# Two networks in one kernel: the sequence and the context taken apart at both borders of the second network's first feed-forward

## The reference

```python
def reference(...):                    # cut
    x = first_block(x, mem, ...)       # retention + differential attention, cross attention, SwiGLU
    return second_block(x, ctx, ...)   # below

def _modnorm(x, g_pre, shift, scale):
    return _rmsnorm(x, g_pre) * (1 + scale) + shift
def _residual(x, y, g_post, gate, weight):
    return x + weight * gate * _rmsnorm(y, g_post)
def _swiglu(h, w1, w3, w2):            # 1024 -> 2816 -> 1024
    return (silu(h @ w1) * (h @ w3)) @ w2

# second_block: m, mc are nine vectors each, silu(c) @ w_ada + b_ada and silu(c_ctx) @ w_ada + b_ada
x     = _residual(x, _swiglu(_modnorm(x, g[0], m[0], m[1]), ffn1...), g[1], m[2], 0.5)
h_ctx = _residual(h_ctx, _swiglu(_modnorm(h_ctx, g[0], mc[0], mc[1]), ffn1...), g[1], mc[2], 0.5)
qa, ka, va, qn, qr, kn, kr, vb, ga, gb = _project(_modnorm(x, g[2], m[3], m[4]), ...)
_, cqa, cka, cva, ...                  = _project(_modnorm(h_ctx, g[2], mc[3], mc[4]), ...)
o_na  = _neighbourhood_attention(qa, ka, va, cka, cva, rpb, n_rows)   # window keys plus all context keys
...                                    # latent attention, gates, output projection
x     = _residual(x, y, g[3], m[5], 1.0)
x     = _residual(x, _swiglu(_modnorm(x, g[4], m[6], m[7]), ffn2...), g[5], m[8], 0.5)
```

## Time and profile before

| | us |
|---|---|
| median of 3 runs | 2569.59 |
| the three runs | 2557.73, 2569.59, 2571.56 |
| the profiled execution | 2560.82 |
| its span, first to last instruction | 2559.0 |
| busy: PE / DVE / ACT / POOL | 2372.7 / 891.6 / 862.8 / 1117.8 |
| mean granted TensorE clock, as a share of full speed | 0.973 |

### The profile page before, as it was taken

How to read it: one execution, slowest core, us unless ns; L and a number is a source line. 1 busy time by engine, 2 the same in 40 slices (tenths; PEclk the granted TensorE clock), 3 DMA queues, 4 the chain that set the end, 5 groups by cost and what they waited for, 6 DMA issues and landing times.

```text
span 2559.0 us, 33468 instructions
## 1 busy us (share of the span) xinstructions
PE 2372.7 (93%) x12008; PEld 1920.3 (75%) x12008; DVE 891.6 (35%) x1492; ACT 862.8 (34%) x1221; POOL 1117.8 (44%) x1352
## 2 busy tenths in 40 slices
PE   5998999878999979999999987999989998999997
PEld 4777677557888868888888866877856875788885
DVE  3332623376667572111110143234124444211113
ACT  3343534333222243311211233155434533422222
POOL 3433355067879763333333342333322033455543
PEclk8999999989999999999999999999999998999998
DMA  3221132234555531121111111122221011222222
GB/s 136 89 74 67 66 103 87 81 138 176 187 184 196 181 116 59 57 75 58 66 58 66 66 58 64 59 87 78 78 70 41 1 66 66 82 99 98 92 98 90
DMA packets 66604, 231.35 MB, mean 90 GB/s; under 512 B 7217, under 2 KB 9521, under 8 KB 66353
## 3 DMA queue, kind: packets, MB, share of 16 engines
q1 hardware_dynamic: 50224, 179.36, 20.1%
q10 hardware_dynamic: 16256, 50.21, 5.7%
HBM read 226.66 MB, written 2.10 MB: 89 GB/s over the span
## 4 chain that ended last, share of the span: by engine, by line
issue 38%; PE 33%; POOL 27%; DVE 1%; POOLq 0%; ACT 0%; DMA 0%; DVEq 0%; ACTq 0%; SPq 0%
PE ps L1405 27%; POOL WLO L293 27%; PE ps L1423 6%; DVE TN L1209 1%; POOLq L246 0%; DVE X L1213 0%; POOLq L291 0%; DVE Y L1235 0%; DMA RAW<-in_stream_dram 0%; PE ps L1474 0%; POOL X L305 0%; DVE TN L896 0%; DVE Y L1233 0%; ACT RS L692 0%; ACT RS L695 0%
## 5 line engine op out<-in xcount | busy, mean ns | idle before, releaser
L293 POOL TENSOR_TENSOR WLO<-RAW,WHI 128x256 fp32r<-128x256 f32 x1340 | 1105.6, 857 | 1399.3 <-ACT WHI L321 1398.5
L321 ACT ACTIVATE WHI<-RAW 128x1024 fp32r<-128x1024 f32 x335 | 354.6, 1059 | 763.1 <-DMA RAW<-in_stream_dram 727.3
L1405 PE MATMUL ps<-HLO,WHI 128*128 128x512 f32 (+2 forms) x1360 | 455.7, 368 | 11.3 <-DVE XK L1068 2.4
L1405 PE MATMUL ps<-HHI,WLO 128*128 128x512 f32 (+2 forms) x1360 | 449.8, 364 | 0.0
L1405 PE MATMUL ps<-HHI,WHI 128*128 128x512 f32 (+2 forms) x1360 | 447.9, 363 | 0.0
L1405 PEld LDWEIGHTS ps<-HLO,WHI 128*128 128x128 f32 (+1 forms) x1360 | 236.3, 188 | 61.2 <-issue 4.9
L1405 PEld LDWEIGHTS ps<-HHI,WHI 128*128 128x128 f32 (+1 forms) x1360 | 235.1, 188 | 44.4 <-issue 3.3
L1405 PEld LDWEIGHTS ps<-HHI,WLO 128*128 128x128 f32 (+1 forms) x1360 | 235.7, 188 | 41.0
L1423 PE MATMUL ps<-HHI,WHI 128*128 128x512 f32 x592 | 204.9, 381 | 52.9 <-POOL WLO L293 30.6
L1131 DVE TENSOR_TENSOR SF<-SF,ps 128x512 f32<-128x512 f32 (+1 forms) x66 | 51.3, 777 | 551.5 <-PE ps L1405 381.9
L1405 PE MATMUL ps<-GLO,WHI 128*128 128x512 f32 x704 | 227.7, 364 | 6.7 <-POOL WLO L293 3.7
(11 more groups left out here) (313 smaller groups left out, 3092.8 us busy)
## 6 DMA issues: line engine op xcount, KB each, us to landing
RAW<-in_stream_dram SPq DMA_DIRECT2D x335, 512.0 KB, 3.3
ADA<-in_ada_dram ACTq DMA_DIRECT2D x72, 512.0 KB, 3.8
BM<-in_bias_dram ACTq DMA_DIRECT2D x8, 448.0 KB, 3.8
DECAY<-in_decay_dram ACTq DMA_DIRECT2D x4, 512.0 KB, 4.2
out_dram<-X SPq DMA_DIRECT2D x8, 256.0 KB, 2.0
X<-in_x_dram SPq DMA_DIRECT2D x2, 512.0 KB, 5.7
X<-in_x_dram ACTq DMA_DIRECT2D x2, 512.0 KB, 6.5
C<-in_mem_dram ACTq DMA_DIRECT2D x1, 1024.0 KB, 5.4
```

Of the source, the lines that this page charges most:

```text
L293: op = nc.gpsimd.tensor_tensor(WLO[:, slot(u), k:k + 2], RAW[:, slot(u), k:k + 2], WHI[:, slot(u), k:k + 2].bitcast(F32), ALU.subtract)
L321: nc.scalar.activation(WHI[:, j], RAW[:, j], ACT.Copy).then_inc(unit_hi, 1)
L1405: mm = nc.tensor.matmul(out, w, x[:, k, tok], start=(k == 0 and n == 0), stop=(k == kt - 1 and n == 2))
```

## The change

At the first border:

- DVE, ACT and TensorE prepare the context's half of norm a0 beside ffn0: squares (ACT) and accumulates (DVE, `ACC0C`) in chunk 0's down part; the sum by one matmul ahead of chunk 1's down part; Ln and Exp, t, high and low in chunk 1's down part and the first three units of chunk 2's. For that the bias and the two coefficient rows of a0 are formed in chunk 0 (`first_coefs`). The two-turn loops of the down parts on ACT and DVE are written out.
- The x half of a0 keeps its temporaries in PSUM banks 4, 6 and 7. TensorE computes the context columns of f1's first three units first, with the sum of a0 behind the first of them, then the x columns of units 0 and 1, then unit 2's x columns together with unit 3 in both widths.
- The other seven coefficient rows and the rest of the bias are formed behind the norm.

At the second border:

- Of f1's last four down units, the x columns of all four are computed first, then the context columns of each; p1's sum for x stands behind the first context part.
- p1 for x is on DVE alone, with temporaries in PSUM; POOL's eight adds are gone. a1 for x follows. The context's p1 and a1 follow those of x on DVE and ACT, beside the matmuls of na_q.
- na_v is placed ahead of na_k, in the weights' order and on TensorE. Its first two units start with the four blocks of x tokens; the context's low halves are waited for ahead of blocks 4 and 5. na_k follows, and the scores wait for three NK copies (the fourth ahead of the second item).

```diff
-          ("xo", 8), ("ffn0", 3 * 22 + 2), ("ffn1", 68), ("na_q", 4), ("na_k", 4), ("na_v", 4),
+          ("xo", 8), ("ffn0", 3 * 22 + 2), ("ffn1", 68), ("na_q", 4), ("na_v", 4), ("na_k", 4),
...
# POOL
-            lows(0, UNIT["na_q"] + AHEAD)
-            for k in range(KD):
-                pool.wait_ge(*norm_at("p1", "p", k + 1))
-                nc.gpsimd.tensor_tensor(X[:, k], X[:, k], TN3[:, k % 2, 0:S], ALU.add).then_inc(s("norm_px"), 1)
-            lows(UNIT["na_q"] + AHEAD, UNITS)
+            lows(0, UNITS)
...
# ACT, beside ffn0's down units m of chunks 0 and 1
+                if at == 0:
+                    nc.scalar.activation(SQ0[:, m], C[:, m], ACT.Square).then_inc(of_ctx("sq"), 1)
+                elif m == 1:
+                    act.wait_ge(*ctx_at("a0c", "ms", 1))
+                    nc.scalar.activation(ps[:, 7, 0:M], ps[:, 7, 0:M], ACT.Ln, scale=1.0 / D, bias=eps).then_inc(of_ctx("ln"), 1)
+                    act.wait_ge(*ctx_at("a0c", "ln", 1))
+                    nc.scalar.activation(ps[:, 7, 0:M], ps[:, 7, 0:M], ACT.Exp, scale=-0.5).then_inc(of_ctx("rs"), 1)
+                elif m >= 3:
+                    first_hi(m - 3)
...
# ACT, second border
+            def ctx_last(j):
+                act.wait_ge(*ctx_at("p1c", "y", j + 1))
+                act.wait_ge(*norm_at("p1", "acc", 5))
+                if j >= 2:
+                    act.wait_ge(*ctx_at("p1c", "acc", j - 1))
+                nc.scalar.activation(SQP[:, j % 2, S:N2], Y[:, 4 + j, S:N2], ACT.Square).then_inc(of_ctx("sq"), 1)
+            root("p1", 6)
+            ctx_last(0)
+            ctx_last(1)
+            convert(UNIT["na_q"])
+            for k in range(KD):
+                act.wait_ge(*norm_at("p1", "x", k + 1))
+                if k >= 2:
+                    act.wait_ge(*norm_at("a1", "ms", k - 1))
+                nc.scalar.activation(SQA[:, k % 2], X[:, k], ACT.Square).then_inc(s("norm_sq"), 1)
+                if k == 2:
+                    convert(UNIT["na_q"] + 1)
+                if k in (3, 5):
+                    ctx_last(k // 2 + 1)
+                if k == 6:
+                    convert(UNIT["na_q"] + 2)
+            root("a1", 4)
...
# DVE, second border
+            ctx_sum(0)
+            ctx_sum(1)
+            dve.wait_ge(*norm_at("p1", "rs", 1))
+            for k in range(KD):
+                ...
+                V.scalar_tensor_tensor(ps[:, 2 * (k % 2)], Y[:, k, 0:S], coef[:, 2, k:k + 1], ps[:, 6], ALU.mult, ALU.mult).then_inc(s("norm_p"), 1)
+                dve.wait_ge(*norm_at("p1", "p", k + 1))
+                V.tensor_tensor(X[:, k], X[:, k], ps[:, 2 * (k % 2)], ALU.add).then_inc(s("norm_x"), 1)
+                if k in (1, 3):
+                    ctx_sum(2 + k // 2)
+            for j in range(4):
+                dve.wait_ge(*ctx_at("p1c", "sq", j + 1))
+                ...
+                V.tensor_tensor(ACCP[:, S:N2], ACCP[:, S:N2], SQP[:, j % 2, S:N2], ALU.add).then_inc(of_ctx("acc"), 1)
...
# TensorE, first border
+            def first1(a):
+                u = UNIT["ffn1"]
+                if a == 0:
+                    pe.wait_ge(*ctx_at("a0c", "lo", KD))
+                    for b in range(3):
+                        pe.wait_ge(s("f0_d"), 2 * KD + 4 + (6, 8, 8)[b])
+                        unit(u + b, 0, [(ps[:, 2 * b + 1, 0:M], ctx_tok)], hi=HHI, lo=HLO, last=False)
+                        if b == 0:
+                            sum_of("a0", ACC0[:], 6)
+                    pair(u, 0, [[(ps[:, 0], x_tok)], [(ps[:, 2], x_tok)]], HHI, HLO, lambda k: [norm_at("a0", "lo", k + 1)])
+                else:
+                    pair(u + 2, 0, [[(ps[:, 4], x_tok)], wide(3)], HHI, HLO, lambda k: [])
# TensorE, second border
+            def last1(u, nt):
+                for j in range(4):
+                    pe.wait_ge(s("f1_d"), 2 * KD + 4 + j + 1)
+                    unit(u + j, 0, [(ps[:, 2 * j], x_tok)], kt=nt, hi=GHI, lo=GLO, last=False).then_inc(of_ctx("up"), 1)
+                for j in range(4):
+                    unit(u + j, 0, [(ps[:, 2 * j + 1, 0:M], ctx_tok)], kt=nt, hi=GHI, lo=GLO)
+                    if j == 0:
+                        pe.wait_ge(s("f1_d"), 3 * KD + 4)
+                        sum_of("p1", ACCP[:, 0:S], 6)
...
+            ctx_total("p1c", ACCP[:, S:N2])
+            query_pair(0)
+            query_pair(2)
+            ctx_total("a1c", ACCC[:])
+            key_value(0, range(4), False)
+            pe.wait_ge(*ctx_at("a1c", "lo", KD))
+            key_value(0, range(4, 6), True)
+            pe.wait_ge(s("nq"), 3)
+            key_value(1, range(6), True)
```

More of the change, by code:

```diff
@@ L235, in norm_at, with ctx_at, of_ctx @@
                     before += 1 if once else tiles + 1 if kind == "acc" else tiles
+        def ctx_at(tag, kind, n):
+            name, before = CTX_SEMS[kind]
+            for norm, counts in CTX_NORMS:
+                if norm == tag:
+                    assert n <= counts[kind]
+                    return s(name), before + n
+                before += counts.get(kind, 0)
+        def of_ctx(kind):
+            return s(CTX_SEMS[kind][0])
         def attend_at(kind, n):
@@ L669, in ffn @@
                                 next_ada(8 + u + 2 * nt - u0 + m, 0)
+                    elif ada:
+                        for m in range(KD):
+                            convert(u + 2 * nt + AHEAD + m)
+                            next_ada(8 + u + 2 * nt - u0 + m, 0)
+                            beside(u - u0, m)
                     else:
@@ new lines, in na_query @@
+            def na_query(a):
+                wait_unit(UNIT["na_q"] + a)
+                nc.scalar.activation(NQ[:, a], ps[:, a], ACT.Copy, scale=0.125).then_inc(s("nq"), 1)
+            convert(UNIT["na_v"])
+            convert(UNIT["na_v"] + 1)
+            na_query(0)
+            na_query(1)
+            ctx_root("a1c")
+            for k in range(KD):
+                act.wait_ge(*ctx_at("a1c", "t", k + 1))
+                nc.scalar.activation(HHI[:, k, S:N2], ps[:, (6, 0)[k % 2], 0:M], ACT.Identity,
+                                     bias=mod[:, 3 * KD + k, 1:2]).then_inc(of_ctx("hi"), 1)
+                if k == 3:
+                    convert(UNIT["na_v"] + 2)
@@ L724, in attend @@
+            convert(UNIT["na_v"] + 3)
+            na_query(2)
+            na_query(3)
             def attend(items, scale, p, pt, on, hi):
@@ new lines, in _ @@
+            dve.wait_ge(s("x_back"), KD)
+            dve.wait_ge(*norm_at("a0", "rs", 1))
+            for k in range(KD):
+                if k >= 2:
+                    dve.wait_ge(*norm_at("a0", "lo", k - 1))
+                V.scalar_tensor_tensor(ps[:, (4, 7)[k % 2]], X[:, k], coef[:, 0, k:k + 1], ps[:, 6], ALU.mult, ALU.mult).then_inc(s("norm_t"), 1)
+                if k:
+                    first_low(k - 1)
+            first_low(KD - 1)
+            add_bias(2 * KD, MOD)
+            dve.wait_ge(s("mod"), 4)
@@ L1258, in attend @@
+            ctx_low(KD - 1)
             def attend(items, scale, on, lo, hi):
@@ L1736, in _, with ffn @@
             sum_of("n3", TN[:, 1])
-            def ffn(tag, u0, outs, x, hid, width, ready):
+            def ffn(tag, u0, outs, x, hid, width, ready, last=None, first=None, side=None):
                 tile0, u = 0, u0
@@ L1765, in ffn, with first_total @@
                         up(i)
-                    for i in range(2):
-                        down(i)
+                    if side:
+                        side(c)
+                    down(0)
+                    if last is not None and nt == CHUNKS[-1]:
+                        last(u + 2 * nt + 4, nt)
+                    else:
+                        down(1)
                     tile0, u = tile0 + nt, u + 2 * nt + KD
+            def first_total(c):
+                if c == 1:
+                    pe.wait_ge(*ctx_at("a0c", "acc", KD + 1))
+                    nc.tensor.matmul(ps[:, 7, 0:M], const[:, ONES], ACC0C[:], start=True, stop=True).then_inc(of_ctx("ms"), 1)
             pe.wait_ge(*norm_at("n3", "rs", 1))
             ffn("f0", UNIT["ffn0"], lambda j: [(ps[:, j], x_tok)], (HHI, HLO), (GHI0, GLO0), S,
-                lambda k: [norm_at("n3", "lo", k + 1)])
+                lambda k: [norm_at("n3", "lo", k + 1)], side=first_total)
             def sums2(tag, tiles, width, sq, first=0, of=None):
```

273 lines of the change are left out of this document (205 added, 68 removed).

## The result

| | us |
|---|---|
| after, median of 4 runs | 2523.80 (2521.05 to 2529.47) |
| before, median of 4 runs | 2570.57 (2557.73 to 2580.05) |
| ratio, 95% interval | 0.9828 (0.9807 to 0.9849) |
| profiled execution of after: time, span, clock | 2529.47, 2527.7, 0.976 |
| a second comparison on another chip, 5 runs | 2527.61 against 2570.82, 0.984 (0.9823 to 0.9857) |

The changed kernel is faster by 1.6 to 1.7%: by the ratios 44 us in the first comparison, 41 in the second (46.8 and 43.2 by the medians). The forecast was 31 us and 2533; the range held. By the two profiled executions alone the difference is 31.3 us, the forecast almost to the microsecond, but that agreement is partly luck, as the experiments show: before's first profile was a low one.

What follows compares the result with a forecast made beforehand. TensorE, busy 93% of the span, sets the length; its idle time at two borders can be won. 10.9 − 0.5 + 20.7 = 31.1 us off 2560.8 gives 2529.7, or 2533.8 from the four-run mean; 2533 forecast, range 2517 to 2555.

Steps and rivals of the forecast that it cites:

- First border, 10.9 us: From ffn0 to f1: context matmuls fill TensorE's idle time, second pair ends at 977.0 instead of 987.9, gain 10.9 us.
- the 1.4 us more: First border: if a table switch costs about 2.66 us, not 1.30, unit 3's weights come 1.4 us later, gain 9.5.
- The side work at 0.5 us: Beside ffn0: context's sum costs TensorE 0.5 us; added DVE adds and ACT table loads fit into idle time, taken as 0.
- The split costs nothing: TensorE: separate 512- and 256-column matmuls take 0.227 and 0.12 us, together 0.347, the same as a step of both.
- Second border, 20.7 us: From f1's last four down units to the scores: scores start at 1628.0 instead of 1648.65, gain 20.7 us.
- the values' wait: Second border, ahead of na_v: TensorE idles 3.4 us for late converted weights, then pays some 1.7 for a low clock.
- The sum, 31.1 us: Whole kernel: 10.9 − 0.5 + 20.7 = 31.1 us gain, from 2560.8 to 2529.7, or 2533.8 from the mean 2564.9.
- rival (b): Fewer waits bite: DVE's first context accumulate not late, or na_v converted in time; gain 41, 2524; chance 0.08.
- (a): More new waits bite in ACT's queue, each costing twice, and PSUM 4 us: gain 16, 2549; chance 0.15.
- (d): Slower: ffn0 becomes bound by POOL, 0.2 us of slack a unit, beside the added DVE work: 2575; chance 0.05.
- (c): TensorE waits for POOL's late weights in f1 after the border, giving the lead back: gain 0 to 10, 2560; chance 0.06.
- The slower rival: Same as (d): ffn0 becomes bound by POOL, slowed by added DVE adds with two SBUF inputs: 2575; chance 0.05.

Runs made afterwards that it cites:

- before_again: The kernel before, unchanged, run once more for a second profile: median 2569.26 us, ratio to before 1.0001.
- before_unrolled: The kernel before with only the two-turn down loops of ffn0 written out on ACT and DVE: median 2567.27 us, ratio to before 1.0004.
- after_again: The changed kernel itself, run again on another chip for a second profile: median 2527.61 us, ratio to before 0.9840.
- more_two_input_adds: The changed kernel plus one unused 512-column DVE add beside each of 16 down units of ffn0's chunks 0 and 1: 2542.87 us, ratio to before 0.9889.
- only_first: The kernel before with the change at the first border alone, p1, a1 and projections as they were: median 2549.42 us, ratio to before 0.9915.

## Why the prediction was right, and where it was off

**First border, 10.9 us: right.** The last matmul of ffn0 to the end of f1's second pair: forecast 35.9, measured 939.0 to 974.8, 35.8, against 46.9 before. The 0.227 us a matmul that the forecast took for the pair holds at a clock of 1.00, and that is what was granted here, with no wait in front. Sum, t, pair and the wait for unit 3 (forecast 1.4, measured 1.17) each came where they were put. The table load ahead of unit 3's convert cost what the earlier trace rows show: it starts at 955.41 and the convert at 956.71, 1.30 us behind, so the 1.4 us more that the prediction set beside it did not come.

**The side work at 0.5 us: the sum was priced too high, and a gain was missed.** The context's sum lengthened chunk 1 of ffn0 by 0.25 us (from its first up to its first down matmul 87.17 before, 87.42 after). But the last eight down units of ffn0 became 1.8 us shorter (39.5 to 37.7 us from the part's first matmul): TensorE's waits for POOL there fell from 3.7 us in all to 2.5. So the side of ffn0 gave 1.6 us where the sum took 0.5 off. That accumulates of 512 columns instead of 768 slow POOL less would fit, but was not tested. The eight more table loads did no visible harm. The idle time of DVE was read in chunk 1 (1.7 us a unit at 819.11); in chunk 0 of the changed kernel there is almost none, and that it sufficed was in part luck.

**The split costs nothing: right for one pace, incomplete.** I took 0.347 for a step of both widths as their sum; it is so, but the alternating stream also has the slower pace of 0.353. The step of 0.36 in the earlier trace rows, taken for rounding, was that: na_k ran at 0.353 in before. f1's first chunk had it in after and not in before, which gave some 3.8 us back in the pair of profiles.

**Second border, 20.7 us: 22.7 measured against the first profile, 25 against the second.** p1's start (forecast 1497.3 with the first border's shift, measured 1497.99), the end of x (1509.3, 1509.8) and ACT's stall (4.5, 5.3) are as worked out. The first q matmul was 2.0 us later than forecast: p1 began 0.7 later, the stall was 0.8 longer, and behind the stall the squares go through two buffers that wait for the sums on TensorE, which I had not counted (a 1.40 us wait ahead of the seventh). The step that failed is the values' wait: 3.4 us and 1.7 for a low clock, measured 0.53 and none. The weights came at the forecast time (1547.3, forecast 1547.5), but the two q pairs ended 2.6 us later than reckoned, so there was hardly a gap, and TensorE's clock did not fall (1.00 from 1547 to 1616). These two misses nearly cancel: the scores came at 1615.94, forecast 1617. Within this border no run takes one part out alone: the overlap, POOL's eight adds that are gone, the temporaries in PSUM and na_v ahead of na_k are told apart by the rows only.

**The sum, 31.1 us, for 44 and 41 measured.** The mechanism was right and the size came out too small, and the base of the sum, one profiled execution of before, was at the low end: 2560.8, against a mean of 2564.9 in the forecast of 2533 and a median of 2570.6 in the result. Three profiles with the old borders (before, before_again, before_unrolled) against two of the changed kernel (after, after_again) differ by 41.6 us on average: 10.6 in border 1, 24.0 in border 2, 3.6 in ffn0, 3.2 in f1's second chunk and third up part, 1.6 behind the scores, less 1.3 ahead of ffn0. The two borders are the change, with the pace of f1's first chunk against it; with the same pace on both sides they give 14 + 24 = 38. The rest is of the kind that moves between profiles of one kernel: 2.8 of ffn0's 3.6 are the one wait for weights (4.53, 7.03 and 5.32 us against 2.79 twice), which was 5.17 and 8.18 in other kernels with the change. So it is not shown that the change causes them, nor that they are chance.

**The rivals.** The median, 2523.80, is the number of rival (b), 2524, but not for its reason. DVE's first context accumulate was late (ACT idled 5.31 us), the values' weights were ready no earlier than forecast, and the scores came 1 us earlier than forecast, not 9.5. More waits biting (a), and POOL at its limit (d), did not happen; that TensorE would wait for weights in f1 after the border (c) did not either. The slower rival named the wrong engine: ffn0's near limit is DVE, as more_two_input_adds shows.

## What to carry to other kernels

Where a norm over two groups of tokens stands between two matmul stages, splitting the groups lets one group's matmuls cover the other's norm. With parts of 512 and 256 columns that cost TensorE nothing here. What has to be followed is each engine's single queue, since a square that waits in the middle of it stalls all behind. A stall found in a trace is still no gain: taking ACT's away shortened its stage by 4 to 6 us and moved no median. Before a forecast is tied to one profile, ask whether the profiled run is typical: two profiles of the same code here were 13 us apart, more than the first border's whole gain. Work moved beside another stage should be priced against that stage's nearest engine, with its idle time per unit written down.

## What was not expected of the hardware

- One alternating stream of 512- and 256-column matmuls runs at 0.347 or 0.353 us a step (201.1 or 205.0 us for 576 steps), at a granted clock of 1.00 in both, and in ten traces kept its pace until the next stall. Computing all 512-column matmuls of a unit first and the 256-column ones after gave 201.6 each time.
- DVE writes its temporaries to PSUM at the pace of SBUF: 0.75 us for 512 columns at 1497.99, as in the earlier trace rows.
- The first dot product of a unit in ffn0 takes 1.75 us at 683.03 in after_again and 1.31 at the same kind of place in before's second chunk (814.37), POOL being busy at both. It takes from 1.16 to 1.80 in before too; over chunk 0's down part its mean is 1.35 in before, 1.38 in before_unrolled and 1.73 in only_first and after_again, so the written-out loops are not the cause. The second dot product is: 1.52 us in before, 1.62 in before_unrolled and after. What sets the first was not tested.
